# The modulation's products as sums along rows on VectorE, its first unit loaded and summed ahead of x

## What is computed

```python
x = layer_norm(x, emb_ln_g, emb_ln_b)
cs = jax.nn.silu(c)
mod = cs @ w_ada[l] + b_ada[l]
sh1, sc1, gt1, sh2, sc2, gt2 = [m[:, None, :] for m in jnp.split(mod, 6, axis=-1)]
h = x * (1.0 + sc1) + sh1
p = h @ w_in[l]
y_a = gmlp_spatial_gating(p[..., :MIX_A], p[..., MIX_A:2 * MIX_A], ...)
y_b = rwkv7_time_mix(p[..., 2 * MIX_A:], ...)
mix = jnp.concatenate([y_a, y_b], axis=-1) @ w_out[l]
x = layer_norm(ALPHA * x + gt1 * mix, ln1_g[l], ln1_b[l])
h = x * (1.0 + sc2) + sh2
gu = h @ w_ffn_in[l]
f = (jax.nn.silu(gu[..., :FFN_HIDDEN]) * gu[..., FFN_HIDDEN:]) @ w_ffn_out[l]
x = layer_norm(ALPHA * x + gt2 * f, ln2_g[l], ln2_b[l])
```

## Time and profile before

| | us |
|---|---|
| median of 3 runs (lowest, highest) | 1429.22 (1426.14, 1432.72) |
| span of the profiled execution | 1428.9 |
| PE, DVE, ACT, POOL busy in it | 1371.8, 698.6, 566.9, 465.6 |
| of it the start to the end of lora0 and k0 | 0 to 59 |
| projections | 60 to 171 |
| chunk stages of g = 0 | 171 to 256 |
| chunk stages of g = 1 | 256 to 317 |
| chain, norms, first of out1 | 317 to 362 |

### The profile page before, as it was taken

The page is one execution under the profiler, slowest core; times in us unless marked ns, Lnnn a source line. Parts: engine busy times, 40 slices in busy tenths (PEclk is TensorE's granted clock), DMA queues, the critical chain, the costliest instruction groups (busy, mean ns, idle before and its releaser), DMA issues.

```text
span 1428.9 us, 23064 instructions
## 1 busy us (share of the span) xinstructions
PE 1371.8 (96%) x9570; PEld 1131.4 (79%) x9570; DVE 698.6 (49%) x1192; ACT 566.9 (40%) x854; POOL 465.6 (33%) x131
## 2 busy tenths in 40 slices
PE   5999999999999999999999999999999999999998
PEld 3788766776788888888888678888798888888886
DVE  6656686464665333353337435687255454453002
ACT  4435654253342223222125445555364433443112
POOL 0243143024314434434522321121212443344344
PEclk9999999998999999999999999999999999999999
DMA  8763266002222232223214420011222223223311
GB/s 333 249 138 118 71 244 220 3 4 84 94 89 89 92 115 89 89 102 134 89 62 164 167 89 31 30 38 53 75 89 89 89 89 114 93 89 109 112 59 59
DMA packets 24741, 147.93 MB, mean 104 GB/s; under 512 B 2716, under 2 KB 3868, under 8 KB 9024
## 3 DMA queue, kind: packets, MB, share of 16 engines
q1 hardware_dynamic: 21128, 134.21, 26.6%
q10 hardware_dynamic: 3512, 12.26, 3.2%
HBM read 141.74 MB, written 4.72 MB: 103 GB/s over the span
## 4 chain that ended last, share of the span: by engine, by line
PE 87%; DVE 7%; ACT 2%; issue 2%; DMA 1%; POOL 1%; SPq 0%; DVEq 0%; ACTq 0%; POOLq 0%
PE bank L2090 24%; PE bank L2092 23%; PE bank L2091 23%; PE bank L2397 5%; PE bank L1168 2%; DMA raw<-in_weights 1%; PE bank L1159 1%; PE bank L1150 1%; DVE xres L1692 1%; PE bank L2276 1%; DVE act_lo L1689 1%; POOL xres L1330 1%; PE bank L2257 1%; DVE bank L1685 1%; PE bank L1077 1%
## 5 line engine op out<-in xcount | busy, mean ns | idle before, releaser
L1301 POOL TENSOR_TENSOR weight_lo<-raw,weight_hi 128x2048 fp32r<-128x2048 f32 (+2 forms) x90 | 415.1, 4612 | 822.9 <-ACT weight_hi L1349 822.8
L2090 PE MATMUL bank<-act_hi,weight_hi 128*128 128x512 f32 (+1 forms) x1136 | 433.1, 381 | 6.0 <-DVE q L879 1.9
L2092 PE MATMUL bank<-act_hi,weight_lo 128*128 128x512 f32 (+1 forms) x1136 | 422.8, 372 | 0.0
L2091 PE MATMUL bank<-act_lo,weight_hi 128*128 128x512 f32 (+1 forms) x1136 | 422.6, 372 | 0.0
L1349 ACT ACTIVATE weight_hi<-raw 128x2048 fp32r<-128x2048 f32 (+1 forms) x98 | 185.2, 1890 | 393.4 <-PE bank L2092 392.3
L2090 PEld LDWEIGHTS bank<-act_hi,weight_hi 128*128 128x128 f32 x1136 | 214.0, 188 | 48.0 <-issue 8.3
L2092 PEld LDWEIGHTS bank<-act_hi,weight_lo 128*128 128x128 f32 x1136 | 213.7, 188 | 38.6
L2091 PEld LDWEIGHTS bank<-act_lo,weight_hi 128*128 128x128 f32 x1136 | 214.1, 188 | 34.7 <-issue 0.5
L2090 PE MATMUL bank<-weight_hi,hid_hi 128*128 128x512 f32 x352 | 136.9, 389 | 0.0
L2091 PE MATMUL bank<-weight_lo,hid_hi 128*128 128x512 f32 x352 | 136.9, 389 | 0.0
L2092 PE MATMUL bank<-weight_hi,hid_lo 128*128 128x512 f32 x352 | 136.9, 389 | 0.0
(11 more groups left out here) (376 smaller groups left out, 1755.3 us busy)
## 6 DMA issues: line engine op xcount, KB each, us to landing
raw<-in_weights SPq DMA_DIRECT2D x120, 1024.0 KB, 4.8
w<-in_w ACTq DMA_DIRECT2D x2, 2048.0 KB, 12.0
bias_rows<-grow ACTq DMA_DIRECT2D x1, 2560.0 KB
xres<-in_x SPq DMA_DIRECT2D x4, 512.0 KB, 5.8
strip<-bias_rows ACTq DMA_DIRECT2D x1, 2048.0 KB, 9.8
out<-xres SPq DMA_DIRECT2D x3, 512.0 KB, 2.6
row_a<-in_ln_g ACTq DMA_DIRECT2D x2, 512.0 KB, 4.1
row_b<-in_ln_b ACTq DMA_DIRECT2D x2, 512.0 KB, 4.9
```

The lines of the kernel that those rows point to most:

```text
L1301: pool.tensor_tensor(wlo[i % SPLIT][:, :size], raw[n % RAW][:, :size], whi[i % SPLIT][:, :size], ALU.subtract).then_inc(lo_ready, 1)
L2090: pe.matmul(o, l[0], r[0], start=first, stop=False)
L2091: pe.matmul(o, l[0], r[1], start=False, stop=False)
L2092: return pe.matmul(o, l[1], r[0], start=False, stop=last)
```

## The change

The modulation is no longer multiplied on PE. The host lays w_ada out transposed, so that a unit holds 2 x 128 output columns as rows, with the 1024 inputs along the free axis. silu(c) is spread over all partitions once: eight small products of a column of silu(c) with ident (`across`), and two ACT copies into `c_row`, 128 x 1024. `ada_sums` on DVE then multiplies each half of a unit by `c_row` and adds up along the row, with the bias as start value; two such instructions make a shift and a scale column.

- ada0_0 is the first unit loaded, ahead of x, and lora0 the second; DVE makes column 0 before it takes up the statistics of x. The other first units follow in the same order as before.
- `affine_hi` is two ACT operations now: scale and offset in the PSUM bank, then the rounding copy; `affine_lo` one DVE operation on the bank. `mod_column(k)` stands behind `affine_lo(k - 1)`.
- The eight second units stand between r0 and pu0 in the load list (ADA_BEHIND), and DVE sums them behind k1, r0, r1, v0 and v1 (ADA_BESIDE).
- The four units of the first gate are loaded ahead of out1_0 and summed in the chunk stages of g = 1; those of the second gate between up1_4 and up1_13. The gate columns are spread to rows by `across` again: `mod_rows` twice in the chain, `gate_rows` at up1_16.
- `ada`, `columns`, `columns_block`, `ada_block`, `mod_columns`, `h_temp`, `bias4` and the entries for them in BESIDE are gone.

```diff
+ADA_BEHIND = {"r0": 1, "r1": 1, "v0": 2, "v1": 1, "pv0": 2, "pv1": 1}
+ADA_BESIDE = {"k1": 1, "r0": 2, "r1": 1, "v0": 2, "v1": 2}
+GATE_AT, GATE_ROWS_AT = (4, 7, 10, 13), 16
...
-    0: {("s", 0): [("ada", 8), ("prep", 2, 0)], ("n", 0): [("ada", 9), ("prep", 2, 1)], ("s", 1): [("ada", 10), ("prep", 2, 5)],
+    0: {("s", 0): [("prep", 2, 0)], ("n", 0): [("prep", 2, 1)], ("s", 1): [("prep", 2, 5)],
...
+    1: {("ta", 1): [("ada", 0)], ("mv", 0): [("prep", 2, 13), ("ada", 1)], ("mv", 1): [("ada", 2)], ("q2", 1): [("ada", 3)],
...
-        if n % 2 and n < 8:
+        if n % 2 and n < 4:
             order.append(("mod_rows", n // 2))
...
         def affine_hi(k):
 
-            await_drained(act, ("cols0", k), "dve")
+            act.wait_ge(S["column_ready"], k + 1)
             await_full(act, ("h1", k))
-            a.done(act.activation(act_hi[:, k, :], bank(("h1", k))[:], ACT.Identity, bias=affine[:, 1, k:k + 1],
-                                  scale=affine[:, 0, k:k + 1]), drain(("h1", k), "act"))
+            full = bank(("h1", k))[:]
+            a.step(act.activation(full, full, ACT.Identity, bias=affine[:, 1, k:k + 1], scale=affine[:, 0, k:k + 1]),
+                   drain(("h1", k), "act"))
+            a.done(act.activation(act_hi[:, k, :], full, ACT.Copy), drain(("h1", k), "act"))
...
+        def ada_sums(name, starts, sums):
+
+            n = UNIT_AT[name]
+            raw_ready(dve, n)
+            for j, (start, total) in enumerate(zip(starts, sums)):
+                w = raw[n % RAW][:, DM * j:DM * j + DM]
+                d.step(V.tensor_tensor_reduce(out=w, in0=w, in1=c_row, scale=1.0, scalar=start, op0=ALU.mult, op1=ALU.add,
+                                              accum_out=total), ada_used if j else None)
+
         def mod_column(k):
...
+            ada_sums(f"ada0_{k}", (col("b_sh1", k), modc[:, k:k + 1]), (affine[:, 1, k:k + 1], scale))
+            ts(affine[:, 0, k:k + 1], scale, col("emb_g", k))
+            stt(affine[:, 1, k:k + 1], scale, col("emb_b", k), affine[:, 1, k:k + 1], ALU.mult, ALU.add, sem=S["column_ready"])
...
+        await_drained(dve, ("c_row", 1), "act")
+        mod_column(0)
         for t in range(TT):
             dve.wait_ge(load[f"x{t}"], 16)
...
         low_part("lora0")
-        for k in range(KC):
+        affine_lo(0)
+        for k in range(1, KC):
             mod_column(k)
...
+        def across(name, column, n):
+
+            for i in range(n):
+                mm = pe.matmul(bank(name)[:, tok(i)], column(i).to_broadcast([P, P]), ident[:], start=True, stop=True)
+            fill(name, mm)
...
             claim(pe, ("mod_rows", j))
-            b = bank(("mod_rows", j))
-            pe.matmul(b[:], ident[:, ROW * j:ROW * j + 1].to_broadcast([P, P]), ada_rows[2], start=True, stop=False)
-            fill(("mod_rows", j), pe.matmul(b[:], ident[0:4, j:j + 1].to_broadcast([4, P]), bias4[:], start=False, stop=True))
+            pe.wait_ge(S["gate_sums"], KC // 2)
+            across(("mod_rows", j), lambda i: gate_cols[:, 0, 4 * j + i:4 * j + i + 1], 4)
```

More of the change, by code:

```diff
@@ L178, in __init__, with add @@
         self.shared = range(4, 8)
-    def add(self, name, bank=None, dve=0, act=0, unit=None, ada=None):
+    def add(self, name, bank=None, dve=0, act=0, unit=None):
         if bank is None:
@@ L184, in add @@
         before = {e: self.drains[e][bank] for e in self.drains}
-        if unit is None and ada is None:
+        if unit is None:
             self.fills[bank] += 1
@@ L266, in plan_banks @@
         dense(f"up1_{m}", drains=[dict(act=1), dict(dve=1)])
+        if m == GATE_ROWS_AT:
+            for j in range(2):
+                b.add(("gate_rows", j), 4 + j, act=1)
     dense_rows("ff1", f"down1_{FT // 2 - 1}")
@@ L1215, in _ @@
         sp.dma_start(pc[:], src["params"]).then_inc(load["params"], 16)
-        for t in range(TT):
-            sp.dma_start(xres[:, t, :], src["x"][0, tok(t), :]).then_inc(load[f"x{t}"], 16)
+        sp.dma_start(ident[:], const("ident")).then_inc(load["ident"], 16)
         for n in range(len(UNITS)):
@@ L1227, in _ @@
             if n == 0:
-                sp.dma_start(ident[:], const("ident")).then_inc(load["consts"], 16)
+                for t in range(TT):
+                    sp.dma_start(xres[:, t, :], src["x"][0, tok(t), :]).then_inc(load[f"x{t}"], 16)
+            elif n == 1:
                 sp.dma_start(bd64[:], const("bd64")).then_inc(load["consts"], 16)
@@ L1626, in _ @@
             ffn_first(m)
+            if m == GATE_ROWS_AT:
+                for j in range(2):
+                    await_full(act, ("gate_rows", j))
+                    a.done(act.activation(acc[:, DM + SEQ * j:DM + SEQ * j + SEQ], bank(("gate_rows", j))[:], ACT.Copy),
+                           drain(("gate_rows", j), "act"))
         for n in range(FT // 2 - 2):
@@ L1739, in affine_lo @@
-            tt(act_lo[:, k, :], full, act_hi[:, k, :].bitcast(F32), ALU.subtract, sem=S["h_lo"])
-        def mod_columns(sums, part, g, b, sh, sc, sem=None):
-            tt(modc[:], sums, pc[:, COLS[sh]:COLS[sh] + 2 * KC], ALU.add, sem=sem)
-            ts(modc[:, KC:], modc[:, KC:], 1.0, op0=ALU.add)
-            tt(affine[:, part, :], pc[:, COLS[g]:COLS[g] + KC], modc[:, KC:], ALU.mult)
-            tt(affine[:, part + 1, :], pc[:, COLS[b]:COLS[b] + KC], modc[:, KC:], ALU.mult)
-            tt(affine[:, part + 1, :], affine[:, part + 1, :], modc[:, 0:KC], ALU.add, sem=S["affine1"])
+            tt(act_lo[:, k, :], bank(("h1", k))[:], act_hi[:, k, :].bitcast(F32), ALU.subtract, sem=drain(("h1", k), "dve"))
@@ L1832, in _ @@
                 prep_side(d, q, part)
+            for _ in range(ADA_BESIDE.get(name, 0)):
+                second_column(next(seconds))
         def pv_norm(t):
```

215 lines of the change are left out of this document (85 added, 130 removed).

## The result

| | median us (lowest, highest) | ratio to before, 95% interval |
|---|---|---|
| before (one run more than in the table of the profile before) | 1427.68 (1424.28, 1432.72) | |
| changed | 1467.76 (1464.14, 1472.92) | 1.0273 [1.0240, 1.0306] |

What follows compares the result with a forecast made beforehand. TensorE was taken as the bound, busy 1371.8 of 1428.9 us. Terms 10.2 + 1.5 + 9 - 9 + 0.5 + 0 + 1 = +13.2, and some 0.8 for early loads, gave 1443 us; range 1425 to 1457.

Steps and rivals of the forecast that it cites:

- Price of a sum: VectorE's multiply-and-add-up along a row: 1.27 us each, 2.96 us for a unit, ends 2.7 and 3.4.
- Part 1, the start: Up to the end of k0: VectorE and ScalarE alternate in turns of 5.3 us, +10.2 us, before the clock.
- +1.5 for the clock: In the start, TensorE's gaps bring some products at half clock: +1.5 us, bounds 0 and 7.
- Part 2, the projections: Second-modulation sums on VectorE collide with POOL and delay the ring's load of pu0: +9 us, some 0.8 for earlier loads.
- 4.8 for the load: In the projections, pu0's load was counted at 4.8 us behind the seventh second unit's sums, landing at 148 to 153.
- TensorE's wait for the square of kk: In the projections, in-order TensorE waits for pair 1's square product, late behind pu0's load: +7.4 to +10.5 us.
- rival D: Start's gaps and the chain run at half clock, +7 and +3 us more: 1453 us, chance .16.
- Part 3: First pairs' chunk stage: 17.0 us of products leave TensorE, only partly gained: -9 us, bounds -7 and -11.
- rival C: Chunk stage and chain, 171 to 362 us: TensorE's relief realised whole, -18 and -10: 1415 us, chance .14.
- Part 4: Serial chain: smaller gate-row products, but TensorE waits for POOL's low part before out1's products: 0 us, range -2.2 to +3.2.
- The gates' sums in the last pairs' stage: Chunk stage of pairs 2 and 3: 10.7 us of sums fall where VectorE waits for products, 0 to +1 us.
- In up1: Up1 stage: eight small products, +0.9 us on TensorE, and four units' sums on VectorE: +1 us with both.

Runs made afterwards that it cites:

- gates-only kernel: Kernel before with only the eight gate units summed on VectorE and gate rows spread by small products; start, projections, second modulation stay on TensorE: 1434.66 us (1.0033).
- two gates-only kernels: That kernel, 1434.66 us, and the same with silu(c)'s row spread in the first pairs' chunk stage and out1 begun where it stood before, 1422.10 us.

## Why the prediction was right in five places and wrong in one

**Price of a sum: right.** I had 1.27 us from three rows; the instruction is the one of the earlier trace rows and takes 1.28, its read-out 0.08, and the period is 1.33. The unit that I had at 2.96 us took 3.1.

**Part 1, the start: right to 1.4 us.** The serial turn was put at 5.3 us and measured 5.37 (act_lo at 36.13, 41.50, 46.87); act_lo(7) ended at 63.67, not 62.7. Behind it stand five groups for which I had 6.8 us; they took 8.7, some at half clock:

```profile
66.42 0.43 PE bank L2107
```

I had +1.5 for the clock, with 7 as the bound, and the 8.7 makes it 1.9. The clock of that stretch fell to 0.73, with waits of 1.4 to 2.4 us ahead of each tile's products. The Trainium skill ("TensorE: Matmul & The Clock Gate", "Why this matters for your kernels") warns of idle gaps between bursts of products; the trace agrees as to the clock, 0.73 in place of 1.00. But the price was 1.9 and not near 7: as long as VectorE set the pace, a slow TensorE cost nothing, and only the tail paid.

**Part 2, the projections: the wrong step.** The mechanism was in the text: the ring has lost its lead, so a load is on the path. The failed step is the price of a load, "4.8 for the load", and with it the 0 to 1.5 us for the earlier loads, which "have a few us in hand each": I had no row for any of them. The 4.8 is a median over 120 loads of the whole run. Two loads that came on the path took 21.3 and 21.1, 33 us more than at that price, and moving the write away took 15.3 us off the stage. Of these two the text doesn't name r1 at all. With most loads at 5 to 8 us the stage loses 13.0 where I had 9.8, and TensorE's wait for the square of kk is 9.3 us where I had 7.4 to 10.5: the rest of the part was near.

A second term was put at nothing without a reason: the clock. My sum has half clock for the start and, in rival D, for the chain, none for the projections. There the products took over 8 us longer in the changed kernel, and still some 3 with the write moved.

**Part 3: right.** -9.2 against -9. The reason fits as well: TensorE was not the bound throughout. The gates-only kernel takes half of the products off TensorE and has 8.7 of the 9.2 already; the other half gives 0.5 more. In the changed kernel the chain of waits to 226 us runs through VectorE's copies and POOL's square, and TensorE waits where the kernel before had fillers and waited 0.7:

```profile
226.02 2.05 PE L2332 MATMUL bank<-sq,bd 128*128 128x512 f32 x2 [4.60 <-POOL sq L1262]
```

So rival C, which needed TensorE to be the bound, is out. That the walk came out at 9 to 0.2 us is in part luck: it left out the clock, which was 0.93 in that stage in place of 1.00.

**Part 4: right.** The chain ended 0.6 later; TensorE stood 7.74 us for POOL where the text has it, at 360.85 in the time of the changed kernel. The gates' sums in the last pairs' stage cost 0.2 here, inside 0 to 1, but 3.0 and 1.2 in the two gates-only kernels, so the 0.2 is not a price to carry on. In up1 1.8, not 1: small, and its cause not looked for.

**The rivals and the range.** D (half clock, 1453) had the place and the price wrong: in the start half clock cost 1.9 and not 7 more, in the chain the clock was 0.78 up to 370 us where it had been 0.67 before, and the place where half clock cost most, over 8 us, was the projections. No rival had the slow loads. The range's upper end took 3 us for the clock where its own bound was 7, but with 7 it would still have been 1461. The load's price had no bound at all: I gave ranges to every sum and to the clock, but took the one number for a transfer as exact.

**Open.** The medians are 40 us apart, the profiled spans 33.4. A run's time is 1.8 us above its span (1464.14 and 1462.3), which the prediction didn't count: so the profiled execution of before stands for a run of 1430.7, 3 us above the median, while that of the changed kernel is the fastest of its four, 3.6 us below. That accounts for the difference, but which stages vary from run to run no trace shows, and in the experiments, too, a difference of medians and one of traces differ by that much: the kernel with the write moved has a median 9 us lower and a span only 1.2 shorter, its profiled execution being the slowest of its four.

## What to carry to other kernels

A transfer has no price of its own: before a load comes on the path, read how long loads take in that very stretch, and what else the DMA engines move there. When a ring of buffers gets more entries, its lead shrinks for all of them; what was hidden in it (here a 2.5 MB write beside which a 4.8 us load takes up to 25) comes out. Look at an instruction order for two operations of the same engine that wait for each other through a third (the start gained 10 us by one swap). With a wait of TensorE's count the slow products behind it, too (here over 8 us beside 20 of waits). And move only the part of the work that falls where its new engine waits: the gates' part of this change, with the row of silu(c) made later and out1 begun as before, is a gain of 0.7%, the whole a loss of 2.7%.

## What the runs showed of the hardware

A transfer of 2.5 MB that spreads eight partitions' rows to DRAM took 56 to 57 us wherever it stood (63 to 119 in the kernel before, 76 to 132 in the changed one, 170 to 227 in the kernel before with the write moved). Its packets took 0.30 to 0.35 of the 16 DMA engines' time in these stretches, and 0.44 in the changed kernel with the write moved, where no load ran beside it. A 1 MB load issued well inside it took 11 to 25 us in these three kernels, against 4.8.

In each of the three kernels that had this write beside the chunk stage TensorE stopped once for 11 to 14 us, for nothing that the profile names but "issue" (until 239.64, 193.69 and, with the sums left out, 227.29 us; 11.07, 11.9 and 13.6 us). Instruction transfers (q8 and one of q14) are the only other traffic around the first of them, 226 to 241 us:

```profile
q10 hardware_dynamic: 325, 0.65, 38.2%
q8 instruction: 2, 0.03, 0.9%
```

I take it for instructions that came late because of the write. The DMA views of the three stops fit: no transfer of q8 starts in the 11 to 19 us before 237, 191 and 224.9 us, then one does, and TensorE goes on within 2.7 us. That the write is what held the transfer back is argued, not shown: no run moved the one without the other.

In the gates-only kernel TensorE waited 3.18 us and came back at half clock (granted clock 0.50 from 65 to 70 us, 1.00 from 70 to 74). The wait and the slow products together are the 5 us that the stage lost.
